# TensorE's branch-free expert code placed in the straight path, from layer 0's first and layer 1's third group of experts on

## What is computed

```python
def hier_moe(h, wg, bg, we, be, w1, w3, w2):
    g_p, g_idx = lax.top_k(softmax(xf @ wg + bg), 1)
    top_v, top_i = lax.top_k(logits_of_that_group, TOP_K)      # TOP_K = 2
    gate = g_p * softmax(top_v)
    ...
    def expert_block(args):
        xb, e = args
        a = jax.nn.silu(xb @ w1[e]) * (xb @ w3[e])             # 1024 -> 512, twice
        return a @ w2[e]                                       # 512 -> 1024
    ...                                                        # y[token] += gate * expert output

for i in range(DEPTH):                                         # DEPTH = 2
    x = x + (pool_mixer, diff_attention)[i % 2](rms_norm(x, norm_mix_g[i]), ...)
    x = x + hier_moe(rms_norm(x, norm_ffn_g[i]), ...)
return rms_norm(x, final_g)
```

## Time and profile before

| what | value |
|---|---|
| median of 3 runs | 1104.18 us (1101.11 to 1104.31) |
| span of the profiled execution | 1099.3 us |
| PE, DVE, ACT busy | 79%, 32%, 21% of the span |
| TensorE clock granted in most slices | 0.9 to 1.0 of full |
| mean rate of all DMA over the span | 388 GB/s |

### The profile page before, as it was taken

The page is one execution under the profiler, slowest core; times in us unless marked ns, Lnnn a source line. Parts: engine busy times, 40 slices in busy tenths (PEclk is TensorE's granted clock), DMA queues, the critical chain, the costliest instruction groups (busy, mean ns, idle before and its releaser), DMA issues.

```text
span 1099.3 us, 18770 instructions
## 1 busy us (share of the span) xinstructions
PE 871.6 (79%) x8132; PEld 512.5 (47%) x8132; DVE 351.2 (32%) x863; ACT 225.6 (21%) x547; POOL 1.2 (0%) x8
## 2 busy tenths in 40 slices
PE   6878776777685868789999988988877766776885
PEld 5744433344343434444787554444534433443442
DVE  3623322323132322222257363322332313232323
ACT  3411211111111111112134332211212111111102
POOL 0000000000000000000000000000000000000000
PEclk9789988989798989999999999999999889897998
DMA  8999999999999999999703678999999999999994
GB/s 343 427 425 424 425 426 427 426 426 427 427 427 427 426 427 427 428 422 421 320 7 120 264 286 361 427 426 426 426 424 425 425 427 427 428 426 427 427 423 191
DMA packets 35587, 426.55 MB, mean 388 GB/s; under 512 B 5394, under 2 KB 6802, under 8 KB 8980
## 3 DMA queue, kind: packets, MB, share of 16 engines
q1 hardware_dynamic: 35476, 424.91, 91.8%
HBM read 423.85 MB, written 1.05 MB: 387 GB/s over the span
## 4 chain that ended last, share of the span: by engine, by line
PE 45%; DMA 38%; DVE 11%; issue 4%; ACT 2%; DVEq 0%; SPq 0%; ACTq 0%
DMA ring<-in_moe_w 37%; PE ps L540 14%; PE ps L588 8%; PE ps L812 5%; PE ps L663 4%; DVE work L1270 3%; PE ps L794 3%; PE ps L473 2%; PE ps L433 2%; PE ps L866 2%; DVE hT L1317 1%; DVE work L1278 1%; PE ps L493 1%; ACT work L986 1%; DVE work L1272 1%
## 5 line engine op out<-in xcount | busy, mean ns | idle before, releaser
L540 PE MATMUL ps<-ring,work 128*32 128x256 f32 x4224 | 284.0, 427 | 137.5 <-DMA ring<-in_moe_w 105.5
L540 PEld LDWEIGHTS ps<-ring,work 128*32 128x32 f32 x4224 | 163.5, 122 | 265.4 <-issue 211.1
L1268 DVE TENSOR_SCALAR work<-work 128x128 f32<-128x128 f32 (+1 forms) x64 | 14.6, 229 | 474.2 <-ACT work L986 474.2
L588 PE MATMUL ps<-ring,work 128*32 128x256 f32 x2032 | 125.2, 388 | 31.6 <-DVE work L1278 30.9
L473 PE MATMUL ps<-work,h_sb 128*128 128x256 f32 x512 | 131.3, 400 | 2.9 <-issue 2.2
L986 ACT ACTIVATE work<-ps 128x256 f32<-128x256 f32 x64 | 24.5, 383 | 504.7 <-PE ps L540 504.7
L1317 DVE COPY hT<-ps 32x512 f32<-32x512 f32 x112 | 76.5, 683 | 133.9 <-PE ps L588 133.1
L473 PEld LDWEIGHTS ps<-work,h_sb 128*128 128x128 f32 x512 | 94.4, 194 | 41.5 <-issue 29.1
L588 PEld LDWEIGHTS ps<-ring,work 128*32 128x32 f32 x2032 | 60.7, 111 | 92.9 <-DVE work L1278 55.5
L998 ACT COPY hT<-ps 32x512 f32<-32x512 f32 x112 | 64.7, 578 | 111.2 <-PE ps L588 110.6
L959 ACT ACTIVATE work<-ps,gcol 128x256 f32<-128x256 f32 (+1 forms) x144 | 58.6, 458 | 110.3 <-PE ps L473 103.9
(11 more groups left out here) (163 smaller groups left out, 467.4 us busy)
## 6 DMA issues: line engine op xcount, KB each, us to landing
ring<-in_moe_w SPq DMA_DIRECT2D x182, 2048.0 KB, 30.5
ring<-in_moe_w SPq DMA_DIRECT2D x15, 1024.0 KB, 30.2
ring<-in_attn_wv SPq DMA_DIRECT2D x2, 2048.0 KB, 33.6
ring<-in_attn_wq SPq DMA_DIRECT2D x2, 2048.0 KB, 32.8
ring<-in_attn_wk SPq DMA_DIRECT2D x2, 2048.0 KB, 33.7
ring<-in_attn_wo SPq DMA_DIRECT2D x2, 2048.0 KB, 36.9
spare<-in_moe_w SPq DMA_DIRECT2D x1, 2048.0 KB, 18.7
x_sb<-in_x SPq DMA_DIRECT2D x2, 512.0 KB, 4.0
```

Source lines behind the costliest of these rows:

```text
L540: mm = pe.matmul(gu_ps[SB * j:SB * (j + 1), b, :, :], xg[:, u, kt, b, k, :], w[:, :, kt, P * j:P * (j + 1)], start=(kt == 0 and b == 0), s ...
L588: mm = pe.matmul(y_ps[SB * i:SB * (i + 1), b, :], actT[:, b, SB * j:SB * (j + 1)], wj[:, 256 * i:256 * (i + 1)], start=(j == 0 and b == 0) ...
```

## The change

`LONG` becomes (0, 2). Layer 0 has no group left that is always long, and layer 1 has two (groups 0 and 1). The test is turned round, so that the short groups stand directly behind it and the long ones in the `Else`. What follows a layer's experts now stands inside each arm, handed over as `rest`: after layer 0's short groups that is the second layer at once, without the load and the test for passes (an expert of at most 32 tokens needs none), and in the `Else` the test and the second layer again. In layer 1 the test for passes stays in both arms. In layer 0 the load and the branch of `other_blocks` are gone from the short arm, and the load and test of the last place of `cnt` stand there instead. DVE computes the last place of `cnt` over more groups, with the same instruction. Nothing changes for ACT and SP.

```diff
-LONG = (2, 4)
+LONG = (0, 2)
...
-            def experts(layer):
+            def experts(layer, rest):
                 u0 = use_before(layer)
-                other_blocks(layer)
...
+                if LONG[layer] > 0:
+                    other_blocks(layer)
                 for gg in range(LONG[layer]):
                     one_group(gg, False)
-
+                pe.wait_ge(s_route, layer + 1)
                 most = pe.value_load(cnt[0:1, NE + NGRP + 1:NE + NGRP + 2], min_val=0, max_val=S)
-                with pe.If(most > SB):
+                with pe.If(most < SB + 1):
+                    for gg in range(LONG[layer], NGRP):
+                        one_group(gg, True)
+                    rest(LONG[layer] > 0)
+                with pe.Else():
+                    if LONG[layer] == 0:
+                        other_blocks(layer)
                     for gg in range(LONG[layer], NGRP):
                         one_group(gg, False)
-                with pe.Else():
-                    for gg in range(LONG[layer], NGRP):
-                        one_group(gg, True)
+                    rest(True)
...
-            experts(0)
...
-                experts(1)
+                experts(1, lambda fuller: more_passes(1))
+
+            def more_passes(layer):
                 most = pe.value_load(cnt[0:1, NE + NGRP:NE + NGRP + 1], min_val=0, max_val=S)
                 with pe.If(most > CAP):
-                    passes(1, most)
...
-            most = pe.value_load(cnt[0:1, NE + NGRP:NE + NGRP + 1], min_val=0, max_val=S)
-            with pe.If(most < CAP + 1):
+                    passes(layer, most)
+
+            def after_first(fuller):
+                if fuller:
+                    more_passes(0)
                 second_layer()
-            with pe.Else():
-                passes(0, most)
-                second_layer()
+
+            experts(0, after_first)
```

## The result

| | us | of |
|---|---|---|
| before, median | 1103.95 (1101.11 to 1104.31) | 4 executions |
| after, median | 1097.63 (1096.98 to 1098.46) | 4 executions |
| ratio after / before | 0.9950, 95% interval 0.9935 to 0.9965 | |
| profiled span, before and after | 1099.3 and 1095.3 | one each |

The changed kernel is faster by 0.5%, 6.3 us by these medians. Measured a second time, with 9 executions, it took 1098.91 us beside 1103.10 for the kernel before (19 executions): ratio 0.9954 (0.9937 to 0.9971), 4.2 us. Forecast were 1102.3 and a range from 1099.8: both are missed on the fast side. The profiled spans differ by 4.0 us, where the sum said 1.9.

The account below looks back on a forecast made before the run. DMA of weights was taken to bound the expert stages, with PE deciding in only a few places. Terms of -0.76, -0.75, 0, -0.4 and 0 sum to -1.9 us, from 1104.18 to 1102.3 us; range 1099.8 to 1106.6.

Parts of the forecast that it names:

- The bound: Expert stages of both layers: DMA of weights sets their end; PE's own time counts in only three places.
- Parts 1 and 2: Layer 0's groups 0 and 1, layer 1's groups 2 and 3: less code read, better weight rate, -0.76 and -0.75 us.
- Part 1's cover: Layer 0's groups 0 and 1: eight ring slots, 39 us of transfers, hide PE's branches, the 3.88 us far one included.
- Part 3: Handover from layer 0 to layer 1: a load and near branch go, worth 0, at most 0.3 us.
- Part 4: Layer 1's groups 0 and 1: code moves, so the third expert's 2.60 us stall may move; -0.4 us, bounds -1.1 to +2.6.
- Part 5: The kernel's end: PE's far jump of 3.9 us stays hidden in some 9 us; 0.
- The base: Whole kernel: the median before, 1104.18 us, was taken as the span plus 4.9 us outside it, before and after.
- Faster: Start of layer 1: both DMA gaps, 1.6 and 1.1 us, close; -4.2 us, 1100.0; chance 0.16.
- stalls at new places: Layer 1's group 0: three stalls of 2.6 us instead of one; +3.7 us, 1107.9; chance 0.12.
- the clock: The two experts at a layer's end: L540 at the lower clock, 1.7 us more each; 1107; chance 0.04.
- far jumps: The kernel's end: nested arms left one by one, three jumps of 3.9 us; +2.4 on the span, 1104.7; chance 0.03.

Follow-up runs that it names:

- pool_code: The changed kernel plus 17 bursts of 256 small GpSimd memsets as straight code in the expert stages; 1109.63 us, ratio 1.0062.
- pool_half: The changed kernel plus 17 bursts of 128 small GpSimd memsets as straight code in the expert stages; 1098.43 us, ratio 0.9958.
- l0_from2b: The changed kernel with layer 0's groups 0 and 1 long again, the old handover test and the second layer in line; 1099.71 us.
- after_again: The changed kernel itself, without an edit, measured a second time; 1098.91 us, ratio 0.9954.
- inline_from24b: The changed kernel with LONG = (2, 4) and the old handover test, short groups and second layer in line; 1101.69 us.
- long_only: The kernel before with only LONG = (0, 2), short groups still in the Else behind the long code; 1107.38 us, ratio 1.0034.
- l0_long2: The changed kernel with LONG = (2, 2), so layer 0's groups 0 and 1 are long again; 1107.59 us, ratio 1.0039.

## Why the prediction was wrong

**The bound was right.** DMA sets the end of both layers: before and after the change, and in pool_code, PE's expert 30 of layer 0 starts 0.13 to 0.14 us behind the last arrival of its chunk.

**Parts 1 and 2: right cause, wrong measure.** Packets of code fell from 17 and 16 to 8 in the two stretches, as counted. Added up packet by packet, the weights' queue had moved the same number of bytes 0.78 us earlier at layer 0's end, and gained 0.85 us more over layer 1 from its second group on; forecast were 0.76 and 0.75. But that is the mean over 16 engines. At "layer 0 ends with the weights, so this is passed on to its end" the step fails: what is passed on is the slowest engine. Its lag fell by 1.3 us in layer 0 and by 2.6 us in layer 1, and with the first engine's place that makes the 1.23 and 2.1 us by which PE got its chunks earlier. So the two terms of 0.76 and 0.75 should have been 1.2 and 2.1. pool_code and pool_half show the mechanism by itself: 33 packets with 0.7 us of transfers cost 12 us, 17 cost nothing. That the lag can also differ by 1.5 us with the same code (l0_from2b in layer 1) means that part of the 2.1 may be where the packets happened to fall; after_again, with a lag of 6.5 us there, says it is not a matter of one execution.

**Part 1's cover: not what it was taken for.** The prediction held a far branch hidden by eight slots of 39 us. For the branch as the kernel before has it in layer 0, behind two groups, that holds (inline_from24b: expert 30 at 473.24 for 473.25 us; 0 to 2.8 us for both layers' branches by the medians). At the first group of layer 0 and the third of layer 1 it doesn't: long_only paid 5.17 and 5.38 us in full, with DMA at 46 GB/s. The change puts its test just there, and what keeps it cheap is the arm that stands in line. The first operation behind the test in the changed kernel, in layer 0 (ahead of the first group) and in layer 1 (ahead of the third), from PE's timeline, shows no idle time at all:

```profile
43.23 3.76 PE L493 MATMUL ps<-work,h_sb 128*128 128x128 f32 x16
46.92 3.72 PE L540 MATMUL ps<-ring,work 128*32 128x256 f32 x64
...
753.65 3.66 PE L540 MATMUL ps<-ring,work 128*32 128x256 f32 x64
```

The prediction priced the placing at nothing because the branch it removed was hidden; it should have priced the branch that the other half of the edit would have made.

**Part 3** was right: layer 0's end came 1.23 us earlier by DMA and the handover itself took the same time. l0_long2 shows what a wrong placing would have cost there, 8.8 us.

**Part 4: the count failed.** The stall stayed in the third expert (2.42 for 2.60 us), against the count of PE's list by 256 instructions after the Trainium skill, "Runtime: NRT & Kernel Launch", Instruction fetch mechanics, by which it should have moved. The Trainium skill says there that a block is 256 instructions, and the packets of 16 KB agree with the size that it gives for one; the runs don't show where a block begins in PE's list, so the count could not be relied on. On PE's side 0.3 us came of Part 4, forecast 0.4: the size fits by luck, since the stall it was to come from stayed. DMA gained hardly anything there. By the mean the weights are 0.7 us earlier at layer 0's end and 1.2 at 660 us, which is layer 1's earlier start, and 1.3 at 755 us.

**Part 5** was right: the last two experts start 3.66 us earlier and the span ends 4.0 us earlier, so no far jump was added behind them.

**The base.** "4.9 us lie outside of the span" was a misreading. Every execution's time is 1.8 us above its own span (after: 1097.07 and 1095.3; after_again: 1096.41 and 1094.6). The profiled execution of before was the shortest of the three that were shown, 1099.3 for 1101.11, and 3 us below the median. The median's gain of 4.2 to 6.3 us scatters around the profiled 4.0 and 4.7 (1099.3 to 1094.6), since executions of one kernel spread over up to 7 us (1101.02 to 1107.92 for the kernel before). The slow products at expert 30 are one source of that spread that the traces show, 1.7 us at a time. The spans of before and of both traces of the changed kernel are free of them, so 4.0 and 4.7 are the cleanest measure of the change. The forecast was 1.9, so the range was not missed by the base alone; but part of the 6.3 us of the first medians is this scatter.

**The rivals.** "Faster" had the right size (1100.0) by the wrong mechanism: neither gap at layer 1's start closed. Its last words, a gain "in a way that rates don't show", are what happened, on the side of DMA. The slower ones (stalls at new places, the clock, far jumps) all stayed away in the changed kernel's traces. Far jumps came true in l0_long2 and long_only. The clock, given a chance of 0.04, is real: 5.35 us for 3.66 at expert 30, as the earlier trace rows had priced it, but it comes in some executions of several kernels and was not brought by the change.

## What to carry to other kernels

Where transfers are spread over 16 engines and a consumer waits for all of a piece, read the arrival of the slowest engine and not the rate: small transfers that fall on one engine, PE's own code among them, cost at least their whole length there (0.64 to 0.83 us for a packet of 0.34 us in pool_code) and stay until the queues run dry. So a short program in a stretch bound by DMA can be worth more than its bytes say. And the arm of a branch that is taken belongs in line with all that follows it. A far jump cost nothing here with seven chunks under way and some 5 us with three, as at the start of a stage. Before spans of single executions are set against each other, look at the clock of the matmuls on the path: here it made differences of up to 3.4 us between executions, which is as much as the change itself.

## What the hardware showed beside that

- A far jump costs more than the 3.88 us of the earlier trace rows: 5.06, 5.17 and 5.38 us in three places of the experiments, with the weights' transfers running before the second and third.
- After such a stop of 5.06 us the next matmuls took 13.51 us in place of 10.54: the slower products cost another 3.0 us, at a granted clock of 0.73.
- GpSimd's code comes in packets of 8 KB (33 for 0.28 MB), PE's in packets of 16 KB (71 for 1.16 MB). The one takes 0.34 us, the other 1.07 us in the trace, and in pool_code one of the first kind put its engine back by 0.64 to 0.83 us.
- Some seven of the 16 engines arrive within 1.7 us of each other in both kernels, and nine lie 4 to 9 us behind the first. From 142 us on GpSimd's packets in pool_code fell on a single engine, as the steps of its lag show.
